# Where the rows of two experts are summed, normed and stored, and how the gate and up weights are loaded

## The chip, the core and the metric

The kernel is one program on one core of a Trainium2 chip. Its time is that of the device for one execution, in microseconds (us). The core has TensorE (PE, matrix products), VectorE (DVE), ScalarE (ACT), GpSimd (POOL) and SyncE (SP), which here only issues transfers. 16 DMA engines carry all transfers; SyncE's go by one hardware queue (q1), GpSimd's indirect ones by a software queue (q0).

## What is computed

Two blocks in a row on 512 tokens of width 1024. The first (attention and a dense layer) and the first half of the second are not touched by the change. What matters is the end: a mixture of 32 experts in 4 groups of 8, and the last norm.

```python
g_p, g_idx = lax.top_k(jax.nn.softmax(g_logits, axis=-1), 1)      # one group per token
e_logits = e_all[jnp.arange(T), g_idx[:, 0]]
e_top, e_idx = lax.top_k(e_logits, TOP_K_IN_GROUP)                # two experts of that group
gate = g_p * jax.nn.softmax(e_top, axis=-1)
...
return (jax.nn.silu(xb @ w_gate[e]) * (xb @ w_up[e])) @ w_down[e] # 1024 -> 256 -> 1024
...
x = x + hier_moe(h2, ...)
return rmsnorm_2(x, norm_f_g)
```

So each token has 1024 / 512 = 2 experts, always of the same group, and its output row is the norm of x + w1 y1 + w2 y2. Each expert's three matrices hold 3 x 1.05 MB.

## The kernel before

**Stages.** Dense products run in chunks of 128 columns; GpSimd makes the second part of each weight chunk. From about 985 us SyncE also loads expert weights; at 1036 us the last chunk is done, the router follows (to 1055 us), then the experts.

**Experts.** They are worked through in 17 units (`UNITS_E`, lines 33 and 34). A unit has 128 rows: 64 of each of two experts. Units 0 to 7 hold experts 0 to 15 in order (`expert_at`, 78). Unit 8 (`EXTRA_AT`) has both halves for one expert: the first one that has more than 64 rows. If that expert's place is 16 or later (`late`, 1728), the unit does all its rows and the order behind it closes up; otherwise it only does the rows over 64, and all the other places must be filled, the last of them by place 18 (`SPARE`), whose weights GpSimd fetches by three indirect transfers (`spare_expert`, 689) with row numbers that are out of bounds, so that nothing is fetched, if `late` is 1 (1778 to 1781). More blocks than one over 64 go through a loop (`for_overflow`, 422) that the profiled execution does not enter.

**One unit.** GpSimd gathers its rows of x (half of x, `scale=0.5` at 1070) from `x_rows` to a buffer of `xe` (682). TensorE turns them, VectorE scales them into `xeT` (1687). TensorE multiplies by gates and ups (2287), ScalarE does silu (1106), VectorE the product with the up half (1694), TensorE turns that (1945) and multiplies by down (2304). `y_of` (1697) adds the weighted product to the row of half an x in `xe`. GpSimd scatters these rows to `y2_rows` (686), which has a row for every token and choice (2 x 512), zeroed earlier.

**Order of the work.** Each engine's order is written out by hand. TensorE puts the first gate products of unit q+1 around turning unit q's hidden rows (2347 to 2363). SyncE (607 to 630) loads gates and ups of a place when the unit six places before has used the buffer (`gate_up_done`), and down weights when the one eight places before has (`down_done`). A gate or up matrix is one transfer of 1 MB, whose rows of 8 KB go to 128 partitions; units 3 and 4 come in quarters with rows of 4 KB (593). GpSimd (705 to 716) waits for y of unit q, scatters it, waits for the scatter of unit q-1, and gathers unit q+4.

**End.** Unit 16 is not scattered. TensorE brings its rows to their tokens with one-hot matrices (`hot`, 2413), SyncE reads all of `y2_rows` back (647), and VectorE and TensorE add the three parts per block of 128 tokens. Then ScalarE squares and sums (1135 to 1144), VectorE refines the root (1164 to 1167) and scales by `gfin` (1877, 1884), and SyncE stores four blocks (651).

**The router's tables.** VectorE finds each row's place; TensorE turns them into lists of rows (`tabi`) and weights (`slotv`) by products with `placed` and `at_row` (2257, 2357). `late_columns` (1730), `place_overflow` (1745) and `name_late_experts` (1766) do so for units 8 to 16 while units 0 to 2 run. `keep_busy` (1956) is filling work of TensorE between these steps.

Of the kernel before, what the change touches and what calls it, by code (L numbers as in the profile page):

```python
# [13 lines left out]
P = 128  # L14
# [15 lines left out]
GU_BUFS, D_BUFS, X_BUFS = 6, 8, 5  # L30
EXTRA_AT = 8
GU_OVER, D_OVER = 0, 6
# [9 lines left out]
def late_at(n):  # L42


    c = (n - 2 * EXTRA_AT + 1) // 2
    return c - 1 if n % 2 else PAIRS - 1 if n == SPARE else c + PAIRS // 2 - 2


def places_of(q):

    return (2 * q, 2 * q + 1) if q < EXTRA_AT else (2 * q,) if q == EXTRA_AT else (2 * q - 1, 2 * q)

# [19 lines left out]
def landings(q):  # L72


    return sum(16 * len([n for n in places_of(j) if n != SPARE]) * (2 if j in PIECED_E else 1) for j in range(q % TURNS, q + 1, TURNS))


def expert_at(n):

    return n if n < 2 * EXTRA_AT else None  # L80
# [155 lines left out]
def gated_blocks(nc, A, out):  # L236
# [8 lines left out]
    with stack:  # L245
# [35 lines left out]
        def const(name, rows=P):  # L281
# [37 lines left out]
                 for n, at in mix_at.items()}  # L319
# [37 lines left out]
            b_at + words([P, X_BUFS - 1, D]), ("picks", [P, 2, NT * NE]), ("at_row", [P, 2 * NT, ROWS]),  # L357
# [7 lines left out]
        tabi, over_n, steps64, over_at, spare_rows, tab_end = lay(low_at + words([P, 2, NK, P]) + words([P, 2, DE]),  # L365
                                       ("tabi", [P, 2, COLS], I32), ("over_n", [1, 2 * OVER + 1], I32), ("steps64", [P, 8]),
                                       ("over_at", [P, 2], I32), ("spare_rows", [P, 1], I32))
        below = place("below", [1, OVER, NE], b_at + words([P, X_BUFS, D]))
# [6 lines left out]
        y2 = place("y2", [P, NT, 2, D], top + 2 * half_buf)  # L375
        x_out = place("x_out", [P, 2, NT, P], base + 4 * CONST_COLS["cos"][0])
        zeros = place("zeros", [P, D], s_at + 2 * half_buf)
        hot = place("hot", [P, NT, P], base + 4 * CONST_COLS["before"][0])
# [9 lines left out]
        y2_rows = nc.dram_tensor("y2_rows", [2 * L, D], F32).ap()  # L388
# [33 lines left out]
        def for_overflow(e, over, block_of):  # L422
            with e.If(over > 1):
                with e.Fori(1, OVER) as i:
                    block_of(i)
                e.wait_ge(S("over_scattered"), 16 * (OVER - 1))
# [13 lines left out]
        def _(sp):  # L440
# [59 lines left out]
            for q in range(QUARTERS):  # L500
# [16 lines left out]
                for n in range(2 * q, 2 * q + 2):  # L517
                    sp.dma_start(y2_rows[n * P:(n + 1) * P, :], zeros[:, :]).then_inc(S("y_zeroed"), 16)
# [123 lines left out]


            for j in range(2):
                sp.wait_ge(S(f"scattered{j}"), 16 * LAST_E // 2)
            for i in range(NT):
                sp.dma_start(y2[:, i, :, :], y2_rows.rearrange("(k t p) n -> t p k n", k=2, p=P)[i])\
                  .then_inc(S(f"block_in{i}"), 16)
            for i in range(NT):
                sp.wait_ge(S("final_out"), i + 1)  # L650
                sp.dma_start(out[i * P:(i + 1) * P, :], y2[:, i, 1, :]).then_inc(S("stored"), 16)
            sp.wait_ge(S("stored"), 16 * NT)
# [3 lines left out]
        def _(pool):  # L656
# [19 lines left out]
            row_bound, slot_bound = pool.to_reg(L - 1), pool.to_reg(2 * L - 1)  # L676
# [8 lines left out]
            def scatter(n, slots, done):  # L685
                pool.indirect_dma_start(y2_rows, bass.IndirectOffsetOnAxis(ap=slots, axis=0), xe[:, n, :], None,  # L686
                                        bounds_check=slot_bound, oob_is_err=False).then_inc(done, 16)
# [13 lines left out]
            for q in range(X_BUFS - 1):  # L701
                gather(q, tabi[:, 1, q:q + 1], S(f"gathered{q}"))
            pool.wait_ge(S("slots_ready"), 1)
            pool.wait_ge(S("y_zeroed"), 16 * 2 * NT)
            for q in range(LAST_E):
                if q == EXTRA_AT - 1:
# [1753 lines left out]
```

## Time and profile before

| what | us |
|---|---|
| median of 3 runs | 1300.85 (1300.69 to 1302.65) |
| the profiled execution | 1302.32 |
| its span, first to last instruction | 1300.0 |
| busy: TensorE, VectorE, ScalarE, GpSimd | 1267.6, 613.1, 460.4, 535.5 |
| weight queue, software queue: share of 16 engines | 45.8%, 1.7% |

Matrix products are pipelined and their ends are modelled, so a busy TensorE is not one at its peak. The shares are averages over stages with different limits; the stage tables below say more. The mean granted clock was 0.994 of full speed.

### The profile page before, as it was taken

To read this page: it belongs to the slowest core of one execution; us is meant where nothing else is said; L and a number is where in the kernel's file an instruction comes from. 1 tells how busy PE (TensorE), PEld (TensorE's weight loads), DVE (VectorE), ACT (ScalarE), POOL (GpSimd) and SP (SyncE) were. 2 spreads that over 40 slices of the span, in tenths; PEclk is the share of its full clock that TensorE was granted. 3 is DMA by queue.
4 is the path that set the end of the run, shared out by engine and by line. 5 is a ranking of instruction groups with operands and counts; after the bars stand their busy time and mean duration, and the time that the engine had idled before them with its cause. 6 is when DMAs were issued, how large, how long until landed. Compare 5 with 4: busy or idle time off the path is not lost.

```text
span 1300.0 us, 18634 instructions
## 1 busy us (share of the span) xinstructions
PE 1267.6 (98%) x6670; PEld 968.7 (75%) x6670; DVE 613.1 (47%) x1162; ACT 460.4 (35%) x770; POOL 535.5 (41%) x685
## 2 busy tenths in 40 slices
PE   8999999999999999999999999999999999999986
PEld 6767777787888888888888788777888875555552
DVE  4868768725542422222225765757243265222225
ACT  5657534435434324133144534145322210000102
POOL 4633323334555655555545664424644211121100
PEclk9999999999999999999999999999999999999999
DMA  7422222112334433434333333312426989999995
GB/s 221 107 65 56 66 58 66 50 49 81 98 96 113 131 97 97 130 98 129 97 98 114 97 93 85 83 49 67 128 81 268 362 323 394 424 421 424 424 423 240
DMA packets 212157, 211.38 MB, mean 163 GB/s; under 512 B 31903, under 2 KB 193425, under 8 KB 200817
## 3 DMA queue, kind: packets, MB, share of 16 engines
q1 hardware_dynamic: 203104, 200.25, 45.8%
q0 software_dynamic: 5184, 8.29, 1.7%
q10 hardware_dynamic: 3796, 1.86, 0.5%
q8 instruction: 46, 0.75, 0.2%
q14 instruction: 27, 0.22, 0.0%
HBM read 205.76 MB, written 16.78 MB: 171 GB/s over the span
## 4 chain that ended last, share of the span: by engine, by line
issue 39%; POOL 31%; PE 26%; DMA 1%; DVE 1%; POOLq 0%; ACT 0%; SPq 0%; DVEq 0%; ACTq 0%
POOL wlo L661 31%; PE bank L2287 8%; PE bank L2304 4%; PE bank L1915 3%; PE bank L1917 3%; PE bank L1916 3%; PE side L1945 2%; DMA y<-y_rows 1%; PE bank L1956 1%; DMA y_rows<-xe,tabi 1%; PE side L1917 1%; PE side L1915 1%; PE side L1916 1%; PE side L2203 1%; PE bank L2419 0%
## 5 line engine op out<-in xcount | busy, mean ns | idle before, releaser
L661 POOL TENSOR_TENSOR wlo<-raw,whi 128x256 fp32r<-128x256 f32 x644 | 498.2, 805 | 524.4 <-ACT whi L785 524.2
L1916 PE MATMUL bank<-actB_lo,whi 128*128 128x512 f32 x608 | 236.7, 389 | 0.0
L1915 PE MATMUL bank<-actB_hi,whi 128*128 128x512 f32 x576 | 227.7, 395 | 0.5 <-POOL wlo L661 0.5
L1917 PE MATMUL bank<-actB_hi,wlo 128*128 128x512 f32 x576 | 224.4, 390 | 0.0
L785 ACT ACTIVATE whi<-raw 128x1024 fp32r<-128x1024 f32 x161 | 169.0, 1051 | 151.8 <-PE bank L1917 124.9
L1915 PE MATMUL bank<-actA_hi,whi 128*128 128x512 f32 x400 | 157.3, 393 | 0.6 <-DVE actA_lo L1201 0.6
L1916 PE MATMUL bank<-actA_lo,whi 128*128 128x512 f32 x400 | 156.1, 390 | 0.0
L1917 PE MATMUL bank<-actA_hi,wlo 128*128 128x512 f32 x400 | 156.1, 390 | 0.0
L2287 PE MATMUL bank<-gu,xeT 128*64 128x256 f32 x1088 | 127.7, 384 | 4.7 <-issue 2.2
L1916 PEld LDWEIGHTS bank<-actB_lo,whi 128*128 128x128 f32 x608 | 114.2, 188 | 24.1 <-issue 1.0
L1915 PEld LDWEIGHTS bank<-actB_hi,whi 128*128 128x128 f32 x576 | 108.1, 188 | 25.9 <-issue 2.3
L1917 PEld LDWEIGHTS bank<-actB_hi,wlo 128*128 128x128 f32 x576 | 108.1, 188 | 22.8
L2287 PEld LDWEIGHTS bank<-gu,xeT 128*64 128x64 f32 x1088 | 80.7, 138 | 46.9 <-issue 15.2
L1938 PE MATMUL bank<-actA_hi,whi 128*128 128x512 f32 x216 | 95.0, 440 | 0.0
L1915 PEld LDWEIGHTS bank<-actA_hi,whi 128*128 128x128 f32 x400 | 75.5, 189 | 17.6 <-DVE actA_lo L1201 1.8
L1916 PEld LDWEIGHTS bank<-actA_lo,whi 128*128 128x128 f32 x400 | 75.5, 189 | 15.8 <-issue 0.2
L1917 PEld LDWEIGHTS bank<-actA_hi,wlo 128*128 128x128 f32 x400 | 75.4, 188 | 15.7
L686 POOL DMA_INDIRECT y_rows<-xe,tabi x16 | 16.3, 1018 | 168.4 <-DVE xe L1702 168.4
L1940 PE MATMUL bank<-actA_hi,wlo 128*128 128x512 f32 x216 | 85.0, 394 | 0.0
L1939 PE MATMUL bank<-actA_lo,whi 128*128 128x512 f32 x216 | 84.4, 391 | 0.0
L1396 DVE TENSOR_SCALAR relu_u<-bank 128x512 f32<-128x512 f32 x32 | 22.1, 692 | 128.7 <-PE bank L1917 128.7
L1106 ACT ACTIVATE hid<-bank,slotv 128x256 f32<-128x256 f32 x17 | 12.6, 740 | 167.8 <-PE bank L2287 167.8
(433 smaller groups left out, 1653.0 us busy)
## 6 DMA issues: line engine op xcount, KB each, us to landing
dn<-in_w_exp_down SPq DMA_DIRECT2D x32, 1024.0 KB, 16.0
raw<-in_w_in SPq DMA_DIRECT2D x57, 512.0 KB, 3.8
gu<-in_w_exp_gate SPq DMA_DIRECT2D x28, 1024.0 KB
gu<-in_w_exp_up SPq DMA_DIRECT2D x28, 1024.0 KB
raw<-in_w_up SPq DMA_DIRECT2D x32, 512.0 KB, 3.9
raw<-in_w_down SPq DMA_DIRECT2D x32, 512.0 KB, 3.6
raw<-in_w_out SPq DMA_DIRECT2D x16, 512.0 KB, 3.7
raw<-in_w_in SPq DMA_DIRECT2D x16, 256.0 KB, 3.1
```

The source lines that it names most:

```text
L661: ins = nc.gpsimd.tensor_tensor(wlo[:, slot, at], raw[:, slot, at], whi[:, slot, at].bitcast(F32), ALU.subtract)
L785: a(whi[:, c % RING, :], raw[:, c % RING, :], ACT.Copy).then_inc(hi_made, 1)
L1396: chain(v.tensor_scalar(relu_u[:, m % 2, :], out_bank(up + m)[:, :], 0.0, None, ALU.max), chunk_freed)
L1915: mm(b[:, :], w_hi, hi[:, k, :], start=first, stop=False)
L1916: mm(b[:, :], w_hi, lo[:, k, :], start=False, stop=False)
L1917: ins = mm(b[:, :], w_lo, hi[:, k, :], start=False, stop=last)
L1938: mm(b[:, :], w_hi, actA_hi[:, k, :], start=k == 0, stop=False)
L1939: mm(b[:, :], w_hi, actA_lo[:, k, :], start=False, stop=False)
L1940: ins = mm(b[:, :], w_lo, actA_hi[:, k, :], start=False, stop=k == NK - 1)
L1945: return nc.tensor.transpose(dst, src, ident[0:src.shape[0], 0:src.shape[0]])
L2287: ins = mm(b[ROWS * h:ROWS * (h + 1), g * DE:(g + 1) * DE], xeT[:, j, k, ROWS * h:ROWS * (h + 1)], gu[n % GU_BUFS][:, g, k, :], start=k == ...
L2304: ins = mm(bank[2 + n][ROWS * h:ROWS * (h + 1), :], hidT[:, j, k * P + ROWS * h:k * P + ROWS * (h + 1)], w[:, k, n * L:(n + 1) * L], start ...
```

## The change

**Who sums.** `x_rows` now holds all of x. A token's two experts lie in units q1 < q2. The unit that comes first scatters x + w1 y1 to `part_rows`, one row a token (512). For the second, GpSimd gathers that row into `xe` over the row of x, once TensorE has turned the latter (`parts_of_unit`); `y_of` adds to it. Then ScalarE squares (`squares_of`), VectorE refines and scales (`finish`), and GpSimd stores the finished rows to `out` (`store_unit`), all within the units, from unit 2 on. A third column of `tabi` lists the rows to finish; the others are out of bounds. The read-back, the one-hot products, `y2` and the sums at the end go. `xe` has 6 buffers instead of 5.

**Order of experts.** So that a token's two experts are two units apart at least, experts go by turns of the groups: place 4 i + g has expert i of group g. Units 8 and 9 (`MIXED_E`) can follow closely on the unit with the other row; for them GpSimd waits for the scatter of the unit just before.

**Weights.** Gates and ups come in two transfers each, along k, with rows of 4 KB. TensorE still waits for the whole of a unit's gates, or ups.

The core of the diff (the overflow loop, which does not run, and the layout of buffers are left out):

```diff
...
-    return n if n < 2 * EXTRA_AT else None
+    return EPG * (n % NG) + n // NG if n < 2 * EXTRA_AT else None
...
+FINISH_FROM = 2
+MIXED_E = (EXTRA_AT, EXTRA_AT + 1)
...
-                    sp.dma_start(gu[n][:, h:h + 1, :, :].rearrange("p h j n -> p h (j n)"), v[:, at_, :])\
-                      .then_inc(loaded[h], 16)
+                    for k in (0, 4):
+                        sp.dma_start(gu[n][:, h:h + 1, k:k + 4, :].rearrange("p h j n -> p h (j n)"),
+                                     v[:, at_, k * DE:(k + 4) * DE]).then_inc(loaded[h], 16)
...
+            def scattered(q):
+                pool.wait_ge(S(f"scattered{q % 2}"), 16 * (q // 2 + 1))
+
+            def parts_of_unit(q):
+                pool.wait_ge(S("xe_used"), 2 * (q + 1))
+                gather_parts(q % X_BUFS, tabi[:, 2, q:q + 1], S(f"parts_in{q % 2}"))
+
+            def store_unit(q):
+                pool.wait_ge(S("rows_finished"), q - FINISH_FROM + 1)
+                store_rows(q % X_BUFS, tabi[:, 2, q:q + 1], S("rows_stored"))
...
             for q in range(LAST_E):
                 if q == EXTRA_AT - 1:
+                    pool.wait_ge(S("slots_ready"), 2)
                     spare_expert()
+                if q:
+                    scattered(q - 1)
+                if FINISH_FROM <= q + 1 < LAST_E and q + 1 not in MIXED_E:
+                    parts_of_unit(q + 1)
                 pool.wait_ge(S("y_made"), q + 1)
                 scatter(q % X_BUFS, tabi[:, 0, q:q + 1], S(f"scattered{q % 2}"))
-                n = q - 1 + X_BUFS
+                n = q + X_FIRST
                 if n < UNITS_E:
...
+                    if q - 2 >= FINISH_FROM:
+                        pool.wait_ge(S("rows_stored"), 16 * (q - 1 - FINISH_FROM))
                     gather(n % X_BUFS, tabi[:, 1, n:n + 1], S(f"gathered{n % X_BUFS}"))
+                if q > FINISH_FROM:
+                    store_unit(q - 1)
+                if q + 1 in MIXED_E:
+                    scattered(q)
+                    parts_of_unit(q + 1)
...
+            parts_of_unit(LAST_E)
+            store_unit(LAST_E - 1)
+            store_unit(LAST_E)
...
+            def squares_of(q):
+
+                one_ = slice(q % NT, q % NT + 1)
+                nc.scalar.preload_act_table_set("natural_log_exp_and_others")
+                for n in range(2):
+                    act.wait_ge(*((S("y_made"), q + 1) if q < LAST_E else (S("last_y_made"), n + 1)))
+                    chain(a(side[3][:, :], xe[:, q % X_BUFS, n * L:(n + 1) * L], ACT.Square, accum_out=gw[:, 10 + n, one_]))
+                    if n == 0:
+                        chain(a(gw[:, 3, one_], gw[:, 10, one_], ACT.Identity, scale=1.0 / D, bias=eps_t[:, :]))
+                chain(a(gw[:, 14, one_], gw[:, 11, one_], ACT.Ln, scale=1.0 / D, bias=gw[:, 3, one_]))
+                chain(a(gw[:, 13, one_], gw[:, 14, one_], ACT.Exp, scale=-0.5), S("guess_made"))
...
                 silu_and_turned(q)
...
+                if q > FINISH_FROM:
+                    squares_of(q - 1)
+                    nc.scalar.preload_act_table_set("silu_and_others")
...
             def y_of(q):
 
                 dve.wait_ge(S("down_done"), q + 1)
+                if q >= FINISH_FROM:
+                    dve.wait_ge(S(f"parts_in{q % 2}"), 16 * ((q - FINISH_FROM) // 2 + 1))
...
+            def finish(q):
+
+                one_ = slice(q % NT, q % NT + 1)
+                dve.wait_ge(S("guess_made"), guesses[0] + 1)
+                chain(v.tensor_tensor(gw[:, 12, one_], gw[:, 10, one_], gw[:, 11, one_], ALU.add))
+                refine(gw[:, 12, one_], gw[:, 13, one_], D, gw[:, 14, one_], gw[:, 15, one_])
+                if q < LAST_E:
+                    dve.wait_ge(S(f"scattered{q % 2}"), 16 * (q // 2 + 1))
+                chain(v.scalar_tensor_tensor(xe[:, q % X_BUFS, :], xe[:, q % X_BUFS, :], gw[:, 13, one_], gfin[:, :],
+                                             ALU.mult, ALU.mult), S("rows_finished"))
...
                 y_of(q)
...
+                if q > FINISH_FROM:
+                    finish(q - 1)
```

VectorE's tables grow with it. Ahead of `values_placed`: which row of a token is first (`apart`, `pos_q`, three operations on `vals`) and the row ids of `placed` for both choices. `late_columns` has 13 operations more, `place_overflow` 7 more, `name_late_experts` some 8 in place of 4; `list_overflow` now comes ahead of the scaling of unit 3's rows. `y2_rows` is zeroed by 8 transfers before, `part_rows` by 4 now.

## Rows read from the trace of the kernel before

**Rows 1.** The page: GB/s in 40 slices of the span.
```profile
GB/s 221 107 65 56 66 58 66 50 49 81 98 96 113 131 97 97 130 98 129 97 98 114 97 93 85 83 49 67 128 81 268 362 323 394 424 421 424 424 423 240
```

**Rows 2.** Busy time by stage: from:to, length, PE, PEld, DVE, ACT, POOL, clock, DMA share, GB/s.
```profile
1180.00:1200.00 20.00, 20.00 (x144) 10.70 (x142) 4.99 (x8) 2.26 (x4) 2.10 (x3) 1.00 1.01 423
...
1240.00:1260.00 20.00, 16.61 (x128) 10.34 (x124) 3.84 (x6) 2.12 (x4) 0.99 (x1) 1.00 1.01 425
```

**Rows 3.** Timeline of the tail: start, duration, engine, line, operation (us).
```profile
1269.46 3.67 PE L2287 MATMUL bank<-gu,xeT 128*64 128x256 f32 x32 [0.33 <-DMA gu<-in_w_exp_up]
...
1274.78 1.28 ACT L1130 ACT_TABLE_LOAD   x1
...
1276.99 0.75 DVE L1854 SCALAR_TENSOR_TENSOR xe<-bank,slotv,xe 128x512 f32<-128x512 f32 x1 [3.15 <-PE bank L2404]
...
1278.71 0.75 DVE L1854 SCALAR_TENSOR_TENSOR xe<-bank,slotv,xe 128x512 f32<-128x512 f32 x1 [0.97 <-PE bank L2404]
...
1287.29 1.28 DVE L1877 SCALAR_TENSOR_TENSOR y<-y,gw,gfin 128x1024 f32<-128x1024 f32 x1
...
1293.29 0.60 ACT L1142 ACTIVATE xe<-bank 128x512 f32<-128x512 f32 x1 [0.42 <-PE bank L2419]
...
1295.42 1.54 DVE L1884 SCALAR_TENSOR_TENSOR y<-bank,gw,gfin 128x512 f32<-128x512 f32 x2
```

**Rows 4.** Chain of work that ended last, in the tail: start, duration, what.
```profile
1267.41 7.44 DMA y_rows<-xe,tabi
...
1275.89 10.13 DMA y<-y_rows
```

**Rows 5.** Transfers that write out, over the span.
```profile
DMA to landing us min/median/max: 2.6/2.6/2.7
```

**Rows 6.** Transfers that write or read y_rows, over the span.
```profile
DMA to landing us min/median/max: 4.8/7.9/12.1
```

**Rows 7.** DMA queues and issues from 1100 to 1200 us: packets, MB, share.
```profile
q1 hardware_dynamic: 5257, 38.31, 90.9%
q0 software_dynamic: 2720, 3.86, 10.3%
...
dn<-in_w_exp_down SPq DMA_DIRECT2D x12, 1024.0 KB, 22.3
```

**Rows 8.** The page: the software queue over the whole span.
```profile
q0 software_dynamic: 5184, 8.29, 1.7%
```

**Rows 9.** Busy time by 4 us, columns as in the second group.
```profile
1056.00:1060.00 4.00, 3.49 (x33) 2.80 (x34) 3.62 (x14) 0.00 (x0) 0.00 (x0) 1.00 0.43 148
...
1084.00:1088.00 4.00, 4.00 (x30) 1.91 (x28) 1.49 (x3) 0.00 (x0) 0.48 (x1) 1.00 1.02 412
1088.00:1092.00 4.00, 4.00 (x38) 2.60 (x35) 2.88 (x12) 0.37 (x1) 2.22 (x2) 1.00 1.04 424
```

**Rows 10.** Timeline of the routing stage.
```profile
1048.39 4.29 PE L1956 MATMUL bank<-ones 128*128 128x128 f32 x36
...
1052.06 0.43 DVE L1661 TENSOR_TENSOR placed<-picks,vals 128x256 f32<-128x256 f32 x1
```

**Rows 11.** Timeline of units 0 and 1: VectorE and TensorE.
```profile
1072.03 1.41 DVE L1702 SCALAR_TENSOR_TENSOR xe<-bank,slotv,xe 128x512 f32<-128x512 f32 x2 [2.09 <-PE bank L2304]
...
1079.48 1.08 PEld L2357 LDWEIGHTS side<-placed,at_row 128*64 128x64 f32 x32 [0.29 <-DVE placed L1764]
```

**Rows 12.** Timeline of GpSimd about units 5 and 6.
```profile
1136.48 1.01 POOL L686 DMA_INDIRECT y_rows<-xe,tabi  x1 [9.75 <-DVE xe L1702]
...
1148.57 1.01 POOL L686 DMA_INDIRECT y_rows<-xe,tabi  x1 [9.76 <-DVE xe L1702]
...
1151.21 0.99 POOL L696 DMA_INDIRECT gu<-in_w_exp_gate,spare_rows  x1 [0.31 <-issue]
```

**Rows 13.** Timeline of SyncE about units 8 and 9.
```profile
1166.92 0.85 SPq L538 DMA_DIRECT2D dn<-in_w_exp_down  x2
1182.01 1.45 SPq L533 DMA_DIRECT2D gu<-in_w_exp_gate  x2
```

More of the change, by code:

```diff
@@ L641, in _ @@
             for_overflow(sp, over, overflow)
[L644 to L652, printed above, removed]
+            sp.wait_ge(S("rows_stored"), 16 * (UNITS_E - FINISH_FROM))
         @block.gpsimd
@@ L1613, in _ @@
             chain(v.tensor_scalar(two, rest, 1.5, None, ALU.is_lt))
[L1614 removed]
+            chain(v.tensor_tensor(picks_r[:, 0:NT, :].rearrange("p t (e g) -> p t g e", g=NG), of_group, by_group(two), ALU.mult),
                   S("picks_made"))
@@ L1643, in _ @@
             chain(v.tensor_tensor(gw[:, 6, :], gw[:, 5, :], gw[:, 4, :], ALU.subtract), S("shifted"))
-            second_rows = placed[:, NT:2 * NT, 0, 0:LATE]
-            chain(v.scalar_tensor_tensor(second_rows, picks8[:, NT:2 * NT, 0:LATE], float(L), second_rows, ALU.mult, ALU.add))
+            firsts, seconds = slice(0, NT), slice(NT, 2 * NT)
+            for mine, other, after in ((firsts, seconds, ALU.is_lt), (seconds, firsts, ALU.is_gt)):
+                chain(v.scalar_tensor_tensor(vals[:, mine, 0], apart, 0.0, pos_q[:, other], after, ALU.mult))
+            chain(v.scalar_tensor_tensor(vals[:, :, 0], vals[:, :, 0], float(L), row_at[:, :], ALU.mult, ALU.add))
+            chain(v.tensor_tensor(placed[:, :, 0, 0:LATE], picks8[:, :, 0:LATE], every(vals[:, :, 0], LATE), ALU.mult))
             dve.wait_ge(S("exps_made"), 1)
@@ L1707, in _ @@
             column_of, bend = (prod[:, 1, NE * n:NE * (n + 1)] for n in (1, 2))
-            full, late, at_end = (gw[:, n, 0:1] for n in range(3))
+            full, late, at_end, group, shift = (gw[:, n, 0:1] for n in (0, 1, 2, 3, 4))
+            in_turn = prod[:, 1, NE * 3:NE * 4]
+            by_group_of = lambda x: x.rearrange("p (i g) -> p i g", g=NG)
+            group_ids = every_expert[:, 0:NG].unsqueeze(1).broadcast_to([P, EPG, NG])
+            last_group = by_group_of(in_turn)[:, :, NG - 1]
             def count_overflow():
@@ L1763, in place_overflow @@
                                       vals[:, :, 1:3].unsqueeze(3).broadcast_to([P, 2 * NT, 2, EVENS + ODDS]), ALU.mult))
+                turn, last = first_at, at_odd
+                chain(v.tensor_scalar(turn, pos[:, :], EVENS - 0.5, -float(EVENS), ALU.is_ge, ALU.mult))
+                chain(v.tensor_tensor(turn, turn, pos[:, :], ALU.add))
+                chain(v.tensor_scalar(last, turn, float(LAST_E - EXTRA_AT), 1000.0, ALU.is_equal, ALU.mult))
+                chain(v.tensor_tensor(turn, turn, last, ALU.add))
+                for mine, other in ((firsts, seconds), (seconds, firsts)):
+                    chain(v.tensor_tensor(vals[:, mine, 0], turn[:, mine], turn[:, other], ALU.is_gt))
+                chain(v.scalar_tensor_tensor(vals[:, :, 0], vals[:, :, 0], float(L), row_at[:, :], ALU.mult, ALU.add))
                 chain(v.tensor_tensor(in_col, in_col, every(vals[:, :, 0], EVENS + ODDS), ALU.mult), S("over_placed"))
```

246 lines of the change are left out of this document (132 added, 114 removed).

## Prediction

> **What bounds the kernel now.** I read the page's slices first, then tables by stage, then the end of the timeline and of the chain, then the DMA queues. The slices show two regimes: up to about 985 us the engines of the DMA are half idle, and after 1080 us they move 421 to 425 GB/s without a break [rows 1]. The tables say the same per stage: from 1100 to 1260 us the DMA share is 1.01 to 1.02 at 422 to 425 GB/s, while TensorE has 16.6 to 20.0 us of work in 20 [rows 2]. That is the expert stage: 32 experts of 3.15 MB. So from 1080 us on every byte and every packet added before the last weights delays them. The reader should see next that the last up weights release TensorE at 1269.46, and that the kernel needs another 30.5 us to 1300.0 [rows 3]. In that tail the chain goes through the last scatter (7.44 us) and the read-back of 4 MB (10.13 us), then sums, roots and four stores of 2.6 us each, the last from 1297.0 [rows 4, 5]. The change therefore does two things: it shortens a tail of 30.5 us and it puts traffic into a stage that has no room.
>
> **The tail (gain).** The steps to the last y stay: up, hidden, turn, down, y, ending at 1278.71 + 0.75 = 1279.46 [rows 3]. After it came one-hot products, read-back, sums, norm and stores; all go. What is new is read off the old last block: from the start of its last square (1293.29) to its scaling (1295.42) are 2.13 us, and one scaling of 128x1024 takes 1.28 us [rows 3]. So 1279.5 + 2.1 + 1.3 = 1282.9, GpSimd starts the store 0.3 us later, at 1283.2. How long a store of 43 rows takes in an idle machine no row shows; scatters took 4.8 to 12.1 us from issue to landing and the last one, with the queues nearly empty, 7.44 [rows 4, 6]. I take 5.5, near the shortest, since nothing runs beside it. With 0.4 us from the last landing to the end, as now (1297.0 + 2.6 to 1300.0) [rows 3, 5], the end is 1289.1 and the tail 19.6 instead of 30.5: 10.9 us less (8.3 to 11.6 by the landing). GpSimd issues the gather of the last unit's parts only after the store of unit 14, whose rows are ready some 2.5 us after y of unit 15 (1267.1): about 1271.2. With 5 to 7.4 us it lands at 1276 to 1278.6 against the first y at 1276.99: 0.3 us. Net gain 10.6 us. The other additions here hide: ScalarE's squares of unit 15 and two table loads of 1.28 us (one is in [rows 3]) end near 1271, silu then ends near 1271.8, before the up products at 1273.1.
>
> **Bytes and packets in the stage (loss).** What a packet costs is worked out from one stretch of 100 us: the weight queue used 90.9% for 5257 packets and 38.31 MB, the software queue 10.3% for 2720 packets and 3.86 MB [rows 7]. In time of one of 16 engines that is 1454 = 5257 a + 38.31 b and 165 = 2720 a + 3.86 b, so a = 8.3 ns for each packet and b = 36.8 us for each MB (estimates; the rounding of 10.3% leaves a between 7.9 and 8.7). Now the terms:
> (1) Rows. The reference's own router on its inputs gives the counts. Now scatters of units 0 to 14 move 930 rows of 4 KB before the last weights. Afterwards each token's first row is scattered (512 rows), the parts of units 2 to 15 are gathered (469) and units 2 to 13 stored (341): 1322. 392 rows x (8.3 + 151) ns / 16 = 3.9 us.
> (2) Skipped rows. Now 5184 packets moved 8.29 MB, that is 2024 rows of 4 KB [rows 8], where 1024 are gathered and 992 scattered by those counts. The 36 transfers have 128 row packets and 16 more each (36 x 144 = 5184), so a skipped row is a packet too. Counting such packets by transfer up to the last weights gives 3080 now and 6050 afterwards: 2970 x 8.3 / 16 = 1.5 us.
> (3) The spare expert. Expert 16 (the first of group 2) is chosen 89 times, the only count over 64. In the old order it stands at place 16, in unit 8, which handles its two blocks with one copy of the weights; `late` is 1 and the three spare transfers skip. Indeed the 8.29 MB leave no room for them. In the new order its place is 4 x 0 + 2 = 2, in an early unit; `late` becomes 0, unit 8 loads it again, and the expert at the last place (31) comes by the spare transfers: 384 packets of 8 KB, 384 x (8.3 + 301) / 16 = 7.4 us. The diff's lines do not say this; the order of the experts does.
> (4) Halves. 22 experts are loaded whole after 1091 us, 44 transfers, each with 128 packets more: 5632 x 8.3 / 16 = 2.9 us. The rows nearest to it agree: while units 3 and 4 came in pieces with 4 KB rows, 412 GB/s, behind them 424 [rows 9]. That is up to 3%, or 3.3 us of the 109 us that these 46 MB take at 424 GB/s; the lower end is 0.
> The Trainium skill ("DMA: Bandwidth & Descriptors", section Bandwidth) speaks against the halves more strongly: batch to 1 MiB, since a lone transfer of 1 MB reaches 341 GB/s and smaller ones less. By 341 instead of 424 the 46 MB of these transfers would cost about 26 us more. The trace disagrees, since queued pieces of 512 KB moved at 412 GB/s [rows 9]; I do not use it.
>
> **VectorE ahead of the stage.** The table of values waits for `placed`, which ends at 1052.49, and TensorE's filling work ends at 1052.7 [rows 10]. The change adds some five small operations of 0.2 us and swaps one: about 0.95 us later. TensorE waited 0.3 us for the first gather anyway, so unit 0 starts 0.7 us later, and with it the weights of unit 3, which wait for its quarters; the DMA share is 0.43 there [rows 9]. Cost 0.7 us. Next, `late_columns` grows by 13 operations, about 3.2 us, against 2.09 us of idle time before y of unit 0, and `place_overflow` by 7, about 1.4 us; TensorE waits for it already now [rows 11]. So TensorE stalls some 2.5 us more at unit 1. The weights of unit 5 are asked for after unit 2's up products, about 1092, and the DMA share before that is 1.04 [rows 9], so the queue is deep enough or nearly: 0.5 us (0 to 2).
>
> **GpSimd's queue.** It issues four transfers for a unit instead of two, each 1.0 us, in a unit of 12.1 us [rows 6, 12]. New waits stand ahead of others: the parts of unit q+1 wait for the scatter of q-1, with y of q queued behind; that scatter lands in 8 of 12 us. At units 8 and 9 it waits for the scatter of the unit just before, and only then gathers: 8 + 8 us plus issue, against 12. Scatter 7 also stands behind the spare's 3 MB, whose first transfer GpSimd issues at 1151.21 now, 10 us before the scatter of unit 7 [rows 12]. VectorE waits in y for these parts, with hidden(q+1) behind it, and TensorE waits for that. From these landings I get TensorE 8 to 11 us later by unit 11. Does that starve the DMA? Down weights asked for at 1166.9 land some 22 us later, and the next request came at 1182.0: 6 to 7 us of queue were left [rows 7, 13], and the spare and the other extras add some 9 to it. So the queue holds and these stalls cost nothing (0 to 5 us), as TensorE will be 8 to 11 us late and the weights 16.9. ScalarE's squares and its two table loads take about 5.5 us of a gap of 9 us between turn and silu; VectorE's norm about 2.5 us of a similar one: nothing.
> The skill's same page (section Queues, rings and completion order) says an engine takes turns between queues packet by packet. No row here shows what the spare's 8 KB packets do to the other queue; by that rule they would take half the engines for some 15 us, which moves no byte and leaves the sum as it is.
>
> **Sum.** Last weights: 3.9 + 1.5 + 7.4 + 2.9 + 0.7 + 0.5 = 16.9 us later. Tail: 10.6 less. Net +6.3. The profiled execution took 1302.32 (span 1300.0 and 2.3 around it), so 1308.6; the median is 1.47 below the profiled one, so 1307.1.
>
> **The rivals.** (A) DMA runs dry behind units 8 and 9. For it: two dependent landings, up to 12.1 us each [rows 6], and the spare ahead of them. It decides when TensorE comes more than about 15 us late to unit 9. Price about 5 us: 1312.1. (B) The spare is not read, because I misread which expert overflows or what `late` does. Then 7.4 us go: 1299.7. Against it stands the count of 89 and the place 2. (C) Faster: the software queue's packets fit beside the weight queue's. The share of 1.02 counts overlapping packets, so an engine may hold two at once; then terms 1 to 3 vanish (12.8 us) and the result is 1294.3. It decides from the point where extra packets lower no weight bytes. Against it: the total stays at 423 to 425 GB/s whatever the mix. (D) Halves are free: 1304.2.
>
> **Chances.** A measurement of this kernel tells about 0.2% (2.6 us) from no change. Forecast 0.55, A 0.15, B 0.10, C 0.10, D 0.10. The forecast and D lie mostly above 1303.5, with 0.05 below; B splits around 1300. Faster 0.12, same 0.13, slower 0.75. The range runs from B, less 0.7 us for its tail, to A with the long landing in the tail (+2.6): 1299 to 1315. The forecast alone is good for 1304 to 1311.
>
> **What would show it.** The last up weights release TensorE near 1286.4 instead of 1269.5; the tail from there is near 19.6 us. Software traffic rises from 8.3 to about 13.5 MB (1024 rows gathered, 3 x 512 others, 3.15 MB spare), in 66 x 144 = 9504 packets. The whole weight loads take 7168 packets more. Around units 8 and 9 VectorE waits for landings. The forecast is wrong if the spare moves nothing, if the total rate in the stage rises over 425 GB/s, or if the DMA share falls under 1 after 1090 us.

## The result, and the profile after

The median of the kernel after's five fast executions is 1308.7 us (a sixth took 2539.3 us and is left out), with 1301.85 us for the kernel before beside it. The ratio is 1.0054 [1.004, 1.0068], the brackets being the 95% interval: slower by 7.0 us, where 6.3 was forecast. The profiled execution has a span of 1305.6 us, 5.6 more than before. The sum came out nearly right, but two of its terms did not.

The page of after: DMA rate in the 40 slices, then the two queues (packets, MB, share of 16 engines), which answer to [rows 1, 8].

```profile
GB/s 223 104 65 64 67 49 66 50 50 80 110 92 120 114 88 95 124 88 123 98 87 97 91 109 83 78 41 78 123 71 312 347 325 402 416 417 417 415 417 190
q1 hardware_dynamic: 208928, 191.87, 44.4%
q0 software_dynamic: 9504, 13.66, 2.8%
```

The software queue has exactly the 9504 packets forecast and 13.66 MB (13.5 forecast), so the spare expert is indeed read. The weight queue has 5824 packets more than before (203104). The rate from 1080 us on is 416 GB/s instead of 424. The table by stage (columns as in [rows 2]) agrees:

```profile
1180.00:1200.00 20.00, 19.75 (x143) 11.06 (x143) 5.18 (x11) 8.77 (x18) 5.06 (x5) 0.98 1.03 418
1240.00:1260.00 20.00, 17.59 (x140) 11.96 (x137) 7.64 (x15) 7.36 (x14) 6.48 (x6) 1.00 1.03 416
```

The DMA share stays at 1.03, so the stage is still bound by bytes and packets. The end of the timeline (start, us, engine, line, operation, shapes, and in brackets the idle time before it and who ended it), to be read against [rows 3]:

```profile
1278.24 3.67 PE L2380 MATMUL bank<-gu,xeT 128*64 128x256 f32 x32 [0.57 <-DMA gu<-in_w_exp_gate]
1283.22 3.67 PE L2380 MATMUL bank<-gu,xeT 128*64 128x256 f32 x32 [1.31 <-DMA gu<-in_w_exp_up]
1292.47 0.75 DVE L1976 SCALAR_TENSOR_TENSOR xe<-bank,slotv,xe 128x512 f32<-128x512 f32 x1 [0.87 <-PE bank L2497]
1293.31 0.60 ACT L1150 ACTIVATE side<-xe 128x512 f32<-128x512 f32 x1 [0.63 <-DVE xe L1976]
1295.60 1.28 DVE L1767 SCALAR_TENSOR_TENSOR xe<-xe,gw,gfin 128x1024 f32<-128x1024 f32 x1
1297.16 0.98 POOL L687 DMA_INDIRECT out<-xe,tabi  x1 [6.15 <-DVE xe L1767]
```

The last up weights release TensorE at 1283.22, 13.8 us later than 1269.46 [rows 3] (forecast: 16.9 later). TensorE still waits for them, 1.31 us. The tail from there is 22.4 us instead of 30.5 (forecast: 19.6). So 13.8 - 8.2 = +5.6, where the forecast had 16.9 - 10.6 = +6.3: the terms were 3.1 and 2.4 us off, and the misses nearly cancel.

After the last store is issued at 1297.16 nothing is computed, and yet the span lasts another 8.4 us. What SyncE waits for at the end, first in the kernel before, then in the one after (total us, times, longest):

```profile
SPq L245 <- DMA out<-y: 2.3, 1, 2.3
SPq L245 <- PEq L245: 0.2, 1, 0.2
```

```profile
SPq L250 <- DMA out<-xe,tabi: 26.7, 1, 26.7
SPq L250 <- PEq L250: 5.7, 1, 5.7
```

The line L250 is the end of the program, where all engines meet (L245 before). Behind the last landing there are now 5.7 us where there were 0.2. The trace names TensorE's sequencer, but that had long been idle; GpSimd's own records have a closing drain there, from 1299.9, 5.5 us long. In the kernel before the same drain took 3.0 us at 1275.4, beside the read-back.

### The profile page after: what moved, and what is told of

Read it like the earlier page. It is cut to its first block, busy times and chain, and to the rows that moved or that the text cites. A ratio compares the mean times of both kernels' runs of the same rounds, so it can differ in the third digit from the quotient of the medians.

```text
span 1305.6 us, 18970 instructions
## 1 busy us (share of the span) xinstructions
PE 1254.0 (96%) x6642; PEld 960.6 (74%) x6642; DVE 634.7 (49%) x1248; ACT 522.8 (40%) x884; POOL 569.5 (44%) x715
## 3 DMA queue, kind: packets, MB, share of 16 engines
q0 software_dynamic: 9504, 13.66, 2.8%
## 4 chain that ended last, share of the span: by engine, by line
issue 39%; POOL 31%; PE 19%; DMA 4%; DVE 3%; SPq 2%; POOLq 0%; ACT 0%; DVEq 0%; ACTq 0%
POOL wlo L654 31%; PE bank L2380 5%; PE bank L2397 3%; PE bank L2008 3%; PE bank L2010 3%; PE bank L2009 3%; SPq L536 2%; DMA gu<-in_w_exp_up 1%; DMA xe<-part_rows,tabi 1%; PE side L2038 1%; DMA part_rows<-xe,tabi 1%; PE side L2009 1%; PE side L2008 1%; PE side L2010 1%; PE side L2296 0%
## 5 line engine op out<-in xcount | busy, mean ns | idle before, releaser
L2010 PEld LDWEIGHTS bank<-actB_hi,wlo 128*128 128x128 f32 x576 | 108.1, 188 | 22.8
L2010 PEld LDWEIGHTS bank<-actA_hi,wlo 128*128 128x128 f32 x400 | 75.1, 188 | 15.7
L1458 DVE TENSOR_TENSOR ytmp<-bank,rs 128x512 f32<-128x512 f32 x32 | 22.1, 692 | 95.7 <-PE bank L2010 95.7
L2397 PE MATMUL bank<-dn,hidT 128*64 128x512 f32 x256 | 60.6, 617 | 3.4 <-ACT hidT L1142 2.7
```

The costliest lines, as they stand in the source:

```text
L2010: ins = mm(b[:, :], w_lo, hi[:, k, :], start=False, stop=last)
L2397: ins = mm(bank[2 + n][ROWS * h:ROWS * (h + 1), :], hidT[:, j, k * P + ROWS * h:k * P + ROWS * (h + 1)], w[:, k, n * L:(n + 1) * L], start ...
```

## The experiments

All ratios are to the kernel before, run on the same chip in the same batch (medians 1302.17, 1301.54 and 1301.98 us). Three theories were tested. T1: the closing drain is now exposed, since GpSimd issues the last transfer. T2: the order of the experts costs 7.4 us by the spare. T3: the halves cost 2.9 us by their packets, against the rival that they pay.

| kernel | ratio to before | 95% interval |
|---|---|---|
| a0_after, the change again | 1.0064 | [1.005, 1.0078] |
| a2_no_drain | 1.0016 | [1.0007, 1.0025] |
| a3_spare_skipped | 1.0012 | [1.0003, 1.0021] |
| a1_whole | 1.0107 | [1.0091, 1.0122] |
| b1_halves (before + halves) | 1.0027 | [1.0018, 1.0036] |
| b2_spare_read (before + spare) | 1.005 | [1.0034, 1.0065] |
| b3_no_drain (before, no drain) | 0.9998 | [0.9989, 1.0008] |
| a6_swapped_no_drain | 0.9974 | [0.9964, 0.9985] |
| a7_whole_swapped_no_drain | 1.0022 | [1.0013, 1.0031] |
| c1_halves_mid | 0.9965 | [0.9952, 0.9978] |
| c2_whole_mid | 1.0024 | [1.0015, 1.0032] |

**The change again.** The base of the first batch.

> The changed kernel again, as the yardstick of the three beside it. Both theories: about 0.5% over the kernel before (7 us). Last up weights near 1283, the tail some 22 us, of which the last 5.5 us come after the last store has landed.

Measured: 1310.81 us, ratio 1.0064. Its trace has the same tail and later weights:

```profile
1285.02 3.67 PE L2380 MATMUL bank<-gu,xeT 128*64 128x256 f32 x32 [1.30 <-DMA gu<-in_w_exp_up]
```

From there to the end of the span (1307.4) it is 22.4 us again. Of the 1.8 us by which the weights come later than in the first trace of this kernel, 1.5 us are there at y of unit 0 already (1075.51 against 1074.06). So differences of one or two us between single traces are not to be built on.

**T1: without the closing drain.**

```diff
-        block = stack.enter_context(nc.Block())
+        block = stack.enter_context(nc.Block(no_gpsimd_drain=True))
```

> The changed kernel with the closing drain of GpSimd left out of the end of the program (every transfer is still waited for by its semaphore). Theory 1: the 5.7 us for which SyncE waits at the end after the last landing are GpSimd's drain, which the kernel before had behind its read-back; then the time falls by about 5.5 us, all of it after the last store's landing, and the ratio to the kernel before is about 1.001. Rival: the store itself lands late (up to 8 us, as scatters do under load), and the drain only waits for it; then the time stays within 1 us of the changed kernel.

Measured: 1304.34 us, 6.5 us less than the kernel after. Its last store and the wait at the end:

```profile
1298.70 0.98 POOL L687 DMA_INDIRECT out<-xe,tabi  x1 [6.15 <-DVE xe L1767]
SPq L250 <- PEq L250: 0.2, 1, 0.2
```

The store is issued at 1298.70 and the span ends at 1301.8, 3.1 us later instead of 8.4. So the drain cost 5.3 us in the trace, and the last store with the end of the program only 3.1 us where I had taken 5.9. The same edit in the kernel before:

> The kernel before without GpSimd's closing drain. There GpSimd is done at 1275 us and its drain of 3.0 us lies beside the read-back: no change, 1301.5 (within 0.1%). Rival: something of the drain lies behind the last store here too, some 3 to 5 us faster, and then the kernel before could have had this gain as well.

Measured: 1301.23 us, 0.9998 [0.9989, 1.0008]. There the drain was free, so its cost belongs to the change: in it GpSimd issues the last transfer, and its drain starts only when that has landed.

**T2: the spare expert.** First the change without the spare's 3.15 MB (the last expert's rows are then computed with other weights).

```diff
-                chain(v.tensor_tensor(at_end, at_end, late, ALU.mult))
+                chain(v.tensor_tensor(at_end, at_end, ones[:, 0:1], ALU.mult))
```

> The changed kernel with the row numbers of the spare expert's three transfers always out of bounds: the same instructions, but the 3.15 MB are not read, and the 25 rows of that expert are computed with old weights. Theory 1 (the stage is bound by the bytes and packets of all queues): the last up weights come 7.4 us earlier and so does the end. Rival (packets of the software queue fit beside those of the weight queue): no change. Second question: the stalls of TensorE at units 8 and 9 (about 17 us now). Scatter 7 no longer stands behind 3 MB and should land in 8 to 9 us instead of 11.4, so that stall shrinks by 2 to 3 us and the one at unit 9 stays; if these stalls counted, the gain would be 10 us instead of 7.4.

Measured: 1303.77 us, 7.0 us less. Its software queue, and its last up products:

```profile
q0 software_dynamic: 9504, 10.54, 2.3%
1277.88 3.67 PE L2380 MATMUL bank<-gu,xeT 128*64 128x256 f32 x32 [1.32 <-DMA gu<-in_w_exp_up]
```

The packets are the same, 3.12 MB are gone, and the last weights are 5.3 us earlier than in the first trace of the kernel after, 7.1 us earlier than in that of a0_after (1.7 us of these are there at unit 0). The 3.12 MB are 3 x 127 rows of 8 KB: the first row of each of the three transfers is never out of bounds, in the kernel before too, whose software queue has 3 packets of 8 KB beside 2016 of 4 KB. So "nothing is fetched" was not quite so. Now the opposite: the kernel before, made to read the spare, which it does not use.

```diff
-                chain(v.tensor_scalar(at_end, const("row_id")[:, 0:1], 0.5 - SKIP, float(P), ALU.is_ge, ALU.mult))
+                chain(v.tensor_scalar(at_end, const("row_id")[:, 0:1], 0.5 - SKIP, 0.0, ALU.is_ge, ALU.mult))
```

> The kernel before, with the three spare transfers made to move their 3.15 MB (into the spare place, which is unused in this input, so that nothing that is computed changes). The forecast's term 3: 384 packets of 8 KB, 7.4 us: 1309.6 (1308.5 to 1311), last ups near 1277, with a DMA share of 1.02 throughout. Rival 1 (it fits beside the weights, as the sum of shares over 1 might suggest): 1302. Rival 2 (the spare's packets hold back scatter 7 and gather 9 behind them, and TensorE's stall becomes the bound): over 1312, with the DMA share under 1 and TensorE idle by 5 us or more around units 8 and 9.

Measured: 1308.49 us, 7.0 us more (ratio 1.005).

```profile
1175.34 1.98 PE L2287 MATMUL bank<-gu,xeT 128*64 128x256 f32 x8 [9.84 <-issue]
1277.05 3.67 PE L2287 MATMUL bank<-gu,xeT 128*64 128x256 f32 x32 [1.22 <-DMA gu<-in_w_exp_up]
```

The last ups came at 1277.05, 7.6 us later than in [rows 3]. TensorE stalled 9.8 us at 1165 to 1175, but the weights still arrived last: that stall cost nothing. The term of 7.4 us is shown from both sides: 7.0 us each by the measured times, 5.3 to 7.6 us in the traces.

**T3: whole transfers in the changed kernel.**

```diff
-                    for k in (0, 4):
-                        sp.dma_start(gu[n][:, h:h + 1, k:k + 4, :].rearrange("p h j n -> p h (j n)"),
-                                     v[:, at_, k * DE:(k + 4) * DE]).then_inc(loaded[h], 16)
+                    sp.dma_start(gu[n][:, h:h + 1, :, :].rearrange("p h j n -> p h (j n)"), v[:, at_, :])\
+                      .then_inc(loaded[h], 16)
...
```

(Left out: the counts that the semaphores wait for.)

> The changed kernel with gates and ups in one transfer of 1 MB each again, rows of 8 KB. Theory 1 (8.3 ns a packet): 5632 packets fewer in the stage, 2.9 us less. Rival A (halves are free, as the queue is full anyway): no change. Rival B (smaller packets let the software queue's transfers land sooner, and that pays): slower than the changed kernel, with landings of scatters and parts 1 to 3 us longer.

Measured: 1316.62 us, 5.8 us slower than with halves. Theory T3 had the wrong sign here. TensorE's last products, and the scatter of unit 7 with the gather of parts that waits for it (GpSimd's queue; L678 scatters, L682 gathers parts):

```profile
1289.68 7.09 PE L2379 MATMUL bank<-gu,xeT 128*64 128x256 f32 x64
1166.10 1.03 POOL L678 DMA_INDIRECT part_rows<-xe,tabi  x1 [3.81 <-DVE xe L1755]
1185.60 1.03 POOL L682 DMA_INDIRECT xe<-part_rows,tabi  x1 [15.49 <-DMA part_rows<-xe,tabi]
```

The same two in the kernel after:

```profile
1165.24 1.03 POOL L679 DMA_INDIRECT part_rows<-xe,tabi  x1 [5.18 <-DVE xe L1756]
1176.85 1.02 POOL L683 DMA_INDIRECT xe<-part_rows,tabi  x1 [7.93 <-DMA part_rows<-xe,tabi]
```

With rows of 4 KB in the weight queue, the gather could be issued 11.6 us after the scatter; with rows of 8 KB it was 19.5 us. And the end is of another kind: gates and ups run as one block of 7.09 us with no wait for a DMA in front. The weights are there, and TensorE is late. The table from 1160 to 1220 us, the kernel after first, then the one with whole transfers:

```profile
1160.00:1220.00 60.00, 50.92 (x344) 28.80 (x342) 19.47 (x42) 22.45 (x43) 17.25 (x17) 0.91 1.03 418
```

```profile
1160.00:1220.00 60.00, 41.25 (x276) 22.83 (x274) 15.51 (x33) 19.34 (x35) 14.68 (x14) 0.85 1.02 423
```

TensorE works 9.7 us less in this stretch, though the DMA moves more (423 GB/s), and its granted clock is lower on top (0.85 against 0.91; more on that below). Do halves then help any kernel? The kernel before with halves alone:

> The kernel before with the halves alone: gate and up weights in 512 KB transfers with rows of 4 KB. The forecast's term 4: 5632 more packets up to the last weights at 8.3 ns over 16 engines, 2.9 us slower (1305.1 by 1302.2; 1302 to 1305.5), last ups near 1272.4, the rate from 1200 to 1260 us about 416 GB/s instead of 424. Rival (halves help, as they did in the full change, by letting the software queue's rows through): 0 to 6 us faster, 1296 to 1302, with shorter landings of x and y rows than 7.5 and 7.9 us. Rival 2 (ring slots: the issues of halves block SyncE and so the down weights are asked for later): over 3 us slower, with a DMA share under 1 somewhere after 1090 us.

Measured: 1305.33 us, ratio 1.0027, 3.5 us slower (2.3 to 4.7).

```profile
1272.82 3.67 PE L2288 MATMUL bank<-gu,xeT 128*64 128x256 f32 x32 [0.68 <-DMA gu<-in_w_exp_up]
1200.00:1260.00 60.00, 50.70 (x374) 27.98 (x372) 12.75 (x20) 4.52 (x8) 6.79 (x7) 1.00 1.02 420
```

The last ups are 3.4 us later and the rate is 420 instead of 425. So in the kernel before halves cost, about what term 4 said. And yet the rows of the software queue land sooner there too: between 1150 and 1220 us the medians are 8.6 us for gathers and 7.4 us for scatters, against 10.1 and 8.4 in the kernel before. That even brings y of unit 8 forward (1172.54 instead of 1176.05), but where the weights arrive last it gains nothing.

**Is it the spare that makes whole transfers slow?** The spare's three transfers stand in front of scatter 7, so without them whole transfers might gain after all. Two kernels in which expert 16 comes late (the halves of each group change places; then `late` is 1 and only the first of each 128 spare rows is read), both without the drain:

```diff
-    return EPG * (n % NG) + n // NG if n < 2 * EXTRA_AT else None
+    return EPG * (n % NG) + n // NG + EPG // 2 if n < 2 * EXTRA_AT else None
...
+            swapped = ((slice(0, EPG // 2), slice(EPG // 2, EPG)), (slice(EPG // 2, EPG), slice(0, EPG // 2)))
...
```

> The kernel after, with two edits: the two halves of each group's experts change places in the order (expert 16 goes from place 2 to place 18, so `late` is 1 and the three spare transfers skip), and no closing drain of GpSimd. All is computed. Theory (the two costs lie in different stretches and add): 7.0 and 6.5 us less than the kernel after, 1310.8 - 13.5 = 1297.3 (1296 to 1299.5), last ups near 1278, software traffic 10.5 MB, the chain without the drain of 5.5 us: 0.4% faster than the kernel before. The new order costs VectorE some five small operations, about 1 us, ahead of unit 0, which may show as 0.5 us. Rival 1 (unit 9 with two blocks of one expert, and its own scatter behind it, stalls TensorE as much as unit 8's spare did, so nothing of the spare's 7 us comes back): 1303 to 1305. Rival 2 (the drain hid the last store's completion, which now ends the program as late): 1300 to 1303.

> As the run before this one (order of experts swapped, no spare read, no drain), but gate and up weights of units 5 to 16 loaded whole, 1 MB each, as in the kernel before. Theory: whole loads were 5.8 us slower in the full change because TensorE's stalls at units 8 and 9, behind the spare's 3 MB in the software queue, became longer than the slack of the weights (19.2 us instead of 11.4 us from scatter 7 to the next parts). Without the spare in that queue the stalls are shorter, the stage is again bound by bytes and packets, and the whole loads should gain their packets: 2.9 us (0 to 3.3) less than the halves, so 1294.4 (1294 to 1297.5). Rival 1: 8 KB packets delay every landing of the software queue enough to bind even without the spare: equal to or up to 6 us slower than the halves, 1297 to 1303. Which of the two: the longest wait of VectorE for parts (11.0 us with the spare skipped and halves) and the landing of scatter 7.

Measured: with halves 1298.68 us, 0.9974 [0.9964, 0.9985], the first kernel faster than before. The two costs nearly add: 1.0064 less 0.9974 is 11.7 us of 13.5. With whole transfers 1304.7 us, 1.0022: 6 us slower again. My theory that the spare causes it falls. VectorE's wait for parts between 1160 and 1220 us (total, times, longest) and the last products, with halves, then with whole ones:

```profile
DVE xe L1762 <- DMA xe<-part_rows,tabi: 21.0, 2, 11.3
1274.96 7.09 PE L2389 MATMUL bank<-gu,xeT 128*64 128x256 f32 x64
```

```profile
DVE xe L1761 <- DMA xe<-part_rows,tabi: 28.4, 2, 15.1
1284.48 7.09 PE L2388 MATMUL bank<-gu,xeT 128*64 128x256 f32 x64
```

In both kernels the last products wait for no DMA, so TensorE is late in both, and later with whole transfers. Two waits for parts, at units 8 and 9, are 7.4 us longer in sum. When VectorE starts y of a unit shows where the time goes (us; the third line is the difference):

| unit | 7 | 8 | 9 | 10 | 15 |
|---|---|---|---|---|---|
| a6, halves | 1163.30 | 1180.81 | 1198.44 | 1210.31 | 1275.18 |
| a7, whole | 1164.80 | 1187.73 | 1207.33 | 1219.62 | 1284.70 |
| later | 1.5 | 6.9 | 8.9 | 9.3 | 9.5 |

Of the 9.5 us, 7.4 arise at units 8 and 9. The 1.5 us before them are there from unit 1 on, and c1, the fastest kernel below, has them too. The median landings of the software queue between 1150 and 1220 us, with halves, then with whole ones:

```profile
part_rows<-xe,tabi POOLq DMA_INDIRECT x5, 6.7
out<-xe,tabi POOLq DMA_INDIRECT x5, 10.0
```

```profile
part_rows<-xe,tabi POOLq DMA_INDIRECT x4, 9.3
out<-xe,tabi POOLq DMA_INDIRECT x4, 11.4
```

Rows land 1.4 to 2.6 us later beside 8 KB rows, here with only three spare rows in the queue. At units 8 and 9 such landings stand one behind the other (scatter, then parts), and TensorE waits for both.

**Where the halves matter.** If that is the reason, only the transfers in flight from 1160 to 1215 us need be halves, those of units 10 to 13. One kernel has halves there only; the other has them everywhere in this stage but there (`HALVED = (5, 6, 7, 8, 9, 14, 15, 16)`).

```diff
+HALVED = range(10, 14)
...
-                    for k in (0, 4):
-                        sp.dma_start(gu[n][:, h:h + 1, k:k + 4, :].rearrange("p h j n -> p h (j n)"),
-                                     v[:, at_, k * DE:(k + 4) * DE]).then_inc(loaded[h], 16)
+                    size = 4 if q in HALVED else 8
+                    for k in range(0, 8, size):
+                        sp.dma_start(gu[n][:, h:h + 1, k:k + size, :].rearrange("p h j n -> p h (j n)"),
+                                     v[:, at_, k * DE:(k + size) * DE]).then_inc(loaded[h], 16)
...
```

> Order of experts swapped, no spare read, no closing drain, as in the two runs before; gate and up weights in halves only for units 10 to 13, whose transfers are in flight from 1160 to 1215 us, and whole for all the others. Theory W (whole loads cost 6.0 us there because their packets of 8 KB make the software queue's rows land later while TensorE waits for two dependent landings at units 8 and 9; the cost arises in that stretch alone): the stalls stay as short as with halves everywhere, and 15 of the 23 loads of this stage save their packets, 15/23 of the 3.8 us that halves cost in the kernel before, 2.5 us: 1296.2 (1295 to 1298.7). Rival X (TensorE is late in this kernel anyway, and what whole loads cost is spread over all units from 11 on, as every unit now waits for four transfers of the software queue): 1301 to 1304. Told apart by the start of the last unit's up products (about 1278.5 with halves everywhere, 1288.0 with whole ones) and by the units' rhythm between 1220 and 1280.

> The complement of the run before: whole loads for units 10 to 13 only, halves for all the others. Theory W: the stalls around 1170 and 1205 us are as long as with whole loads everywhere, and the end follows TensorE: 1302 to 1305. Rival X: about a third of the 6 us, 1300 to 1301.

Measured: halves in the middle only 1296.34 us, 0.9965 [0.9952, 0.9978]; whole in the middle only 1304.75 us, 1.0024 [1.0015, 1.0032], as slow as whole everywhere (1.0022). Wait for parts and last products, c1 first, then c2:

```profile
DVE xe L1764 <- DMA xe<-part_rows,tabi: 21.0, 2, 11.3
1277.01 3.67 PE L2391 MATMUL bank<-gu,xeT 128*64 128x256 f32 x32 [0.65 <-DMA gu<-in_w_exp_up]
```

```profile
DVE xe L1764 <- DMA xe<-part_rows,tabi: 27.9, 2, 14.1
1282.55 7.09 PE L2391 MATMUL bank<-gu,xeT 128*64 128x256 f32 x64
```

The whole penalty arises in the transfers of four units. With halves there alone, TensorE is back to waiting for weights (0.65 us). Against a6 this kernel is 1.2 us faster by the ratios, where 2.5 was expected of the packets saved; the intervals of the two overlap, so this gain is not shown by itself. Nor could saved packets bring it alone, since a6 ends without waiting for weights. This is the fastest kernel of the study, 0.35% faster than the kernel before.

**The clock as a rival.** Behind long stalls the granted clock of TensorE falls from 2.4 GHz (1.00) to 1.2 GHz (0.50). From 1160 to 1220 us its mean is 0.94 in a6 and c1, 0.86 in a7 and c2. Is the penalty then one of the clock? The stretch behind unit 9 shows what it costs, in a6 first, then in c1:

```profile
1195.00:1205.00 10.00, 5.43 (x38) 3.17 (x35) 5.18 (x11) 2.23 (x3) 3.50 (x3) 0.82 1.03 416
1200.00:1210.00 10.00, 7.23 (x26) 2.81 (x28) 3.66 (x8) 5.18 (x10) 4.52 (x4) 0.66 1.03 422
```

```profile
1195.00:1205.00 10.00, 8.29 (x72) 5.06 (x70) 4.57 (x11) 0.75 (x1) 2.85 (x3) 1.00 1.03 416
1200.00:1210.00 10.00, 8.29 (x58) 4.18 (x56) 5.69 (x12) 5.54 (x11) 3.51 (x3) 1.00 1.03 424
```

In a6 TensorE waited 4.6 us for unit 9's hidden rows, the clock fell, and from y of unit 9 to y of unit 10 it took 11.9 us; in c1 it waited 1.7 us there, the clock stayed, and it took 9.3 us. So the clock can cost 2.6 us at this place. But a7 pays it as a6 does (12.3 us against 11.9), so of their 9.5 us the clock explains only 0.4 at this place, and the table above puts the rest earlier, at the waits for parts. Between c2 and c1, which are 9.8 us apart at y of unit 15, it is 2.7 of them (12.0 against 9.3 us).

What stays open: whether it is the size of the rows itself or how many bytes SyncE has queued (with halves four issues of ups take up to 9.6 us in its queue, whole ones 0.4 us each) that delays the software queue. No run separates the two.

## Why the prediction came out right, and where it was not

**Terms 1 to 4, bytes and packets.** Both queues from 980 us to the last up weights, before (to 1269 us) and after (to 1283 us):

```profile
q1 hardware_dynamic: 19697, 102.79, 87.2%
q0 software_dynamic: 5040, 8.04, 7.5%
```

```profile
q1 hardware_dynamic: 27716, 102.48, 85.0%
q0 software_dynamic: 8793, 12.78, 11.4%
```

That is 11772 packets and 4.43 MB more. By the prices of the prediction (8.3 ns, 36.8 us per MB, over 16 engines) it is 6.1 + 10.2 = 16.3 us; the four terms had 15.7. What did not follow is the time: +13.8.

The mis-sized figure is the price of a packet. As time in the queues it holds: from 1100 to 1260 us the prices give 163.3 us of work for the kernel after, and its queues show 102.3% of 160 us, so 163.7. But these are more than 160, as they are before (161.8, 101.2%), so packets overlap, and where there are more of them they overlap more. Rival C was right in that, though not that terms vanish by it. In time a packet costs less: over this stretch, the packets (11819 to 21089) and MB (66.24 to 67.68) of all thirteen traces fit 160 us = (5.6 ns per packet + 36.9 us per MB) / 16, within 0.5 us (an estimate, by least squares). By it the packets and bytes are 4.1 + 10.2 = 14.3 us, against the 13.8 measured (15.6 in a0_after, of which 1.5 us lie before the stage). Terms 1 and 2 had no run of their own.

The count of term 4 was low as well. b1's weight queue has 211168 packets in all, the kernel before 203104: 8064 more, which is 56 x 144 and not 56 x 128 = 7168, since a second transfer brings 16 packets of its own. So the prediction's 5632 are 6336.

**Term 3, the spare.** Right: 7.4 us forecast, 7.0 us more in the kernel before by its time and 7.6 in the trace, 7.0 less in the changed one. Rival B (not read) is out by 13.66 MB, rival C (it fits beside) by b2.

**Term 4, the halves.** Right in size for the kernel before (2.9 us; b1: 3.5, with 2.3 to 4.7). Wrong as the price of the edit in this change: undone alone, the kernel becomes 5.8 us slower. I had priced each edit by itself and written of the stalls at units 8 and 9 that they "cost nothing (0 to 5 us)", as TensorE would be 8 to 11 us late and the weights 16.9. Measured, y of unit 11 is 13.2 us later (1225.54 against 1212.32) and the weights 13.8: next to nothing was left between them. The stalls cost nothing only because the halves are there. Rival A put its 5 us on the right place, dependent landings at units 8 and 9, but not on the right mechanism: without halves the DMA does not run dry (share 1.02, 420 GB/s from 1220 to 1280 us in a1), TensorE itself ends last. Of the software queue I wrote that turns taken with it move no byte and leave the sum as it is. The Trainium skill ("DMA: Bandwidth & Descriptors", section Queues, rings and completion order) says an engine changes between queues only after a whole packet. The landings agree in direction: scatter 7 to parts 11.6 us beside 4 KB rows and 19.5 beside 8 KB rows. An estimate from rows of this case, which takes it that each packet of the small queue lets one row of the other go first (no run shows that): a transfer has 144 / 16 = 9 packets an engine, and each behind one weight row of 8 KB instead of 4 KB waits 301 - 151 = 150 ns longer, so 1.4 us a transfer; a6 and a7 differ by 1.4 to 2.6. The Trainium skill's rule that I did not use, to batch to 1 MiB ("DMA: Bandwidth & Descriptors", section Bandwidth), has the sign of b1, though 3.5 us there are far from the estimated 26; in the changed kernel it would have been wrong by sign as well: the kernel with 512 KB transfers is the faster one, though the rate falls from 423 to 418 GB/s.

**VectorE ahead of the stage, and the stall at unit 1.** The rows turned up as forecast: unit 0 starts at 1055.91, 1.0 us later than before (0.7 forecast). TensorE's idle time before the product over the table at unit 1:

```profile
1082.94 1.17 PE L2450 MATMUL side<-placed,at_row 128*64 128x72 f32 x31 [2.58 <-DVE placed L1855]
```

2.58 us, as forecast. The price of 0.7 + 0.5 us for both did not show, since packets and bytes alone give 14.3 of the 13.8 us: by the prices above, the engines of the DMA left 22.8 us unused between 980 and 1080 us in both kernels. What was asked for later in one slice was made up in another: between 1056 and 1060 us the share is 0.71 instead of 0.43 [rows 9].

**The tail.** The compute steps were right: y ended 10.0 us after the release (10.0 forecast), the scaling began 2.4 us after that (2.1), and the store was issued at its end. The two last terms failed. The landing of the last scatter with its end took 3.1 us (a2), not 5.9: I had taken it from scatters beside other traffic; with nothing beside it, it was nearer to the 2.6 us of the plain stores [rows 5]. And the drain, 5.3 us, was in no row that I read: before, it lay beside the read-back. I had asked what is late next on each engine's work, but not what the program itself does at its end. In sum 8.4 us from issue to end instead of 5.9.

**The rivals' chances.** D (halves are free) is excluded by b1. The drain is a mechanism that no rival had; it moved the result by 5.3 us towards slower, the earlier weights (3.1) and the shorter landing (2.8) by 5.9 the other way. That the sum came out within 1 us is therefore luck; what was foreseen and shown is the sign, the spare, and that the last weights set the end.

## What to carry to other kernels

When the last transfer of a kernel changes its issuer, look at what that engine does at the end of the program: GpSimd's closing drain was free beside other work and 5.3 to 6.5 us behind it. Two queues that share the DMA engines must be priced together: in three pairs of kernels the rows of the small queue landed sooner when the busy one was loaded in halves, and where dependent landings stand one behind the other, that can be worth more than the packets cost. Make them small only there (c1), and test an edit of a joint change both by undoing it in the new kernel and by doing it alone in the old one: here the two answers had opposite signs.

## What the hardware showed unexpectedly

- GpSimd's closing drain took 3.0 us in the kernel before (36 indirect transfers) and 5.5 us in the one after (66), in the raw records; whether it grows with their number was not tested. It was as long (5.5 us) with whole transfers (a1) and without the spare (a3).
- Beside a weight queue with 8 KB rows, indirect transfers of up to 128 rows of 4 KB landed in 9.3 to 11.4 us (medians of a7), beside 4 KB rows in 6.7 to 10.0 (a6), at a total DMA share of 1.02 to 1.03 in both.
- A skipped row of an indirect transfer is still a packet, of 4 bytes in the trace's records: the software queue has 9504 packets with the spare read and without (after and a3), and 381 of them change from 8 KB to 4 bytes.
- Packets overlap on a DMA engine: at a price of 8.3 ns each as time in the queues, they cost 5.6 ns in time where the engines are full (an estimate, from the fit above).
- Where TensorE had waited 4.6 us for unit 9's hidden rows, the granted clock then fell to 1.2 GHz in part (mean 0.66 from 1200 to 1210 us, a6), and the unit took 11.9 us; where it had waited 1.7 us, the clock stayed at 1.00 and the unit took 9.3 us (c1).
- With nothing else in the queues the last indirect store, issued by GpSimd at 1298.70, was done and the program ended 3.1 us later (a2), where loaded ones took 4.8 to 12.1 [rows 6].
